# Hybrid encoder trunk on one core: in the dense heads, values copied out and normed in their own step, scaling moved ahead of the next combination, and a wait added to GpSimd's weight pieces

## What is computed

```python
def attend(q_blk):                                  # diff_attention, 128 queries at a time
    s = jnp.einsum('bqhcd,bkhcd->bhcqk', q_blk, k).astype(jnp.float32) * scale
    s = jnp.where(key_ok, s, NEG)
    p = jax.nn.softmax(s, axis=-1)
    a = p[:, :, 0] - lam * p[:, :, 1]
    return jnp.einsum('bhqk,bkhv->bqhv', a.astype(v.dtype), v)
...
    ob = diff_attention(qb, kb, vb, lam, valid)
    ob = rms_norm(ob, subln_w.reshape(B_HEADS, B_V_DIM)) * (1.0 - lam_init)
    yb = ob.reshape(bsz, lp, B_WIDTH).astype(dt) * jax.nn.silu(gb)
```

## Time and profile before

| | us |
|---|---|
| median of 3 runs | 1924.39 |
| lowest and highest run | 1917.27, 1925.56 |
| profiled execution, its own time | 1919.49 |
| its span | 1918.2 |
| busy: TensorE / VectorE / ScalarE / GpSimd | 1716.1 / 1107.8 / 878.5 / 406.7 |
| dense passes, layer 0 (B3 within) | about 570 to 875 (803 to 875) |
| dense passes, layer 1 (B3 within) | about 1506 to 1808 (1742 to 1808) |

### The profile page before, as it was taken

The page is one execution under the profiler, slowest core; times in us unless marked ns, Lnnn a source line. Parts: engine busy times, 40 slices in busy tenths (PEclk is TensorE's granted clock), DMA queues, the critical chain, the costliest instruction groups (busy, mean ns, idle before and its releaser), DMA issues.

```text
span 1918.2 us, 35760 instructions
## 1 busy us (share of the span) xinstructions
PE 1716.1 (89%) x13754; PEld 1591.9 (83%) x13754; DVE 1107.8 (58%) x2533; ACT 878.5 (46%) x2652; POOL 406.7 (21%) x390
## 2 busy tenths in 40 slices
PE   3799999999889899878989989999998888887896
PEld 3798899999888788668989989999998878775796
DVE  6475584445447777763185846834553575666516
ACT  4434545345416666572053444352552365546603
POOL 5430221220111102010463103113103101112044
PEclk9899999999989999899999999999998899999998
DMA  7200100200120111233031001011001111113312
GB/s 252 66 24 12 56 23 28 74 26 10 34 75 14 37 32 36 64 109 106 23 111 57 23 13 55 23 50 51 29 10 60 47 26 34 45 26 121 118 46 89
DMA packets 97705, 102.44 MB, mean 53 GB/s; under 512 B 7488, under 2 KB 87600, under 8 KB 97280
## 3 DMA queue, kind: packets, MB, share of 16 engines
q1 hardware_dynamic: 96576, 99.08, 16.0%
q10 hardware_dynamic: 960, 1.07, 0.2%
HBM read 70.43 MB, written 21.17 MB: 48 GB/s over the span
## 4 chain that ended last, share of the span: by engine, by line
PE 69%; DVE 16%; ACT 8%; issue 3%; POOL 2%; DMA 1%; SPq 0%; DVEq 0%; ACTq 0%
PE psum L855 45%; PE psum L995 6%; ACT p_b L1440 4%; PE psum L930 3%; PE psum L1142 3%; PE psum L1049 3%; DVE row_max L1909 3%; PE psum L1126 2%; DVE p_b L1923 2%; PE psum L1035 1%; DVE hbuf L1582 1%; ACT p_b L1438 1%; ACT aT_b L1450 1%; DVE stats L1575 1%; POOL w_lo L821 1%
## 5 line engine op out<-in xcount | busy, mean ns | idle before, releaser
L855 PE MATMUL psum<-w_hi,hT_hi 128*128 128x256 f32 x1824 | 529.6, 290 | 6.1 <-POOL w_lo L821 4.1
L855 PE MATMUL psum<-w_hi,hT_lo 128*128 128x256 f32 x1824 | 517.3, 284 | 0.0
L855 PE MATMUL psum<-w_lo,hT_hi 128*128 128x256 f32 x1824 | 516.8, 283 | 0.0
L817 POOL CAST w_hi<-w_raw 128x512 fp32r<-128x512 f32 (+1 forms) x168 | 112.7, 671 | 1354.9 <-DMA w_raw<-in_w_in 804.5
L855 PEld LDWEIGHTS psum<-w_hi,hT_hi 128*128 128x128 f32 x1824 | 348.0, 191 | 14.7 <-POOL w_lo L821 4.9
L855 PEld LDWEIGHTS psum<-w_lo,hT_hi 128*128 128x128 f32 x1824 | 348.1, 191 | 0.0
L855 PEld LDWEIGHTS psum<-w_hi,hT_lo 128*128 128x128 f32 x1824 | 348.1, 191 | 0.0
L855 PE MATMUL psum<-hT_hi,w_hi 128*128 128x346 f32 (+1 forms) x672 | 230.8, 343 | 24.2 <-DVE hT_lo L1568 9.3
L855 PE MATMUL psum<-hT_hi,w_lo 128*128 128x346 f32 (+1 forms) x672 | 222.2, 331 | 0.0
L855 PE MATMUL psum<-hT_lo,w_hi 128*128 128x346 f32 (+1 forms) x672 | 221.7, 330 | 0.0
L821 POOL TENSOR_TENSOR w_lo<-w_raw,w_hi 128x512 fp32r<-128x512 f32 (+1 forms) x168 | 211.3, 1258 | 34.4 <-DVE neg_max L1910 23.0
(11 more groups left out here) (161 smaller groups left out, 2661.7 us busy)
## 6 DMA issues: line engine op xcount, KB each, us to landing
w_raw<-in_w_in SPq DMA_DIRECT2D x72, 256.0 KB, 3.7
w_raw<-in_w_in SPq DMA_DIRECT2D x28, 512.0 KB, 4.2
h_dram<-hbuf SPq DMA_DIRECT2D x16, 512.0 KB, 2.6
w_raw<-in_w_out SPq DMA_DIRECT2D x16, 512.0 KB, 4.1
hbuf<-h_dram SPq DMA_DIRECT2D x16, 512.0 KB, 5.5
qk_b<-y_dram SPq DMA_DIRECT2D x16, 512.0 KB, 3.2
y_dram<-y_stage SPq DMA_DIRECT2D x96, 64.0 KB, 1.6
qk_t<-rot SPq DMA_DIRECT2D x56, 86.5 KB, 2.1
```

The source lines that it names most:

```text
L817: pool.tensor_copy(hi, raw).then_inc(w_hi_done, 1)
L855: last = nc.tensor.matmul(out_ap, lhs[a](k), rhs[b](k), start=k == 0 and a + b == 0, stop=k == KT - 1 and b == 1)
```

## The change

Three edits. On ScalarE, `norm` of step t now follows `values_out` of the same step, where before `norm` of t-1 stood ahead of it. On VectorE, `finish` of t-1 now stands ahead of `combine` of t+1 in all passes; in B3 it has also moved ahead of `lo_of_rows`. On GpSimd, the first operation of a piece tied to a pass now also waits for the combination of step j.

```diff
@@ gpsimd, beside_maximum
             step = b_step(l, head, n, 1)
             if c == 0:
+                pool.wait_ge(b_comb, B_STEP[l, head, n])
                 wait_filled(pool, ("s", l, *step, 1))
@@ scalar, pass_b
             def norm(step):
-                if step is None:
-                    return
                 g, t = step
...
-                norm(b_step(l, g, t, -1))
                 values_out(t)
+                norm((g, t))
                 if nx and t == q_tiles(l) - 2:
                     meta_out(l, nx)
                 if not nx and t >= Y_LAG:
                     hi_of_rows("y", l, t - Y_LAG)
-            if not nx:
-                norm((g, q_tiles(l) - 1))
@@ vector, pass_b
                 for x in made:
                     qk_rope(l, nx, x)
-                if not nx:
-                    if t > Y_LAG:
-                        lo_of_rows("y", l, t - 1 - Y_LAG)
-                    finish(b_step(l, g, t, -1))
+                finish(b_step(l, g, t, -1))
+                if not nx and t > Y_LAG:
+                    lo_of_rows("y", l, t - 1 - Y_LAG)
                 if after:
                     combine(after)
-                if nx:
-                    finish(b_step(l, g, t, -1))
```

## The result

The changed kernel takes 1893.07 us, the median of 4 runs (1886.95 to 1896.57). The kernel before, run beside it, takes 1922.57 (4 runs, 1917.27 to 1925.56). The ratio is 0.9846, with an interval from 0.9811 to 0.9881: 1.2 to 1.9% faster. The profiled execution took 1886.95 us with a span of 1885.6, 32.6 less than the span before. The forecast was 1901, with 1895 to 1907 as its own bounds and 1893 to 1910 as the range. So the direction was right and the gain larger than the sum said: 29.5 us between the medians instead of 23.4.

The account below looks back on a forecast made before the run. TensorE bounds steps with projections, rotations the ends of B1 and B2, a VectorE-ScalarE ring B3 and late B0. Gains of 7.8, 2.6, 7.7, 2.0 and 2.4 sum to 22.5 us, giving 1897.0 or 1901.9; forecast 1901, bounds 1895 to 1907, range 1893 to 1910.

Parts of the forecast that it names:

- the 0.44 us for L1910 beside a piece: B3, three pieces with a scaling, both layers: GpSimd's cast delays this tiny VectorE operation by 0.44, making steps 7.2 us.
- the 7.41 given to the first step of y's loop: B3 from step 4 on: every step that makes y takes 7.41 us, bounded by 6.95 and 7.7.
- the 0.4 for each late step of B0: B0: each late step gains 0.4 us, or 0.2 where rotations fill VectorE; B0 together 2.4.
- the hand-overs: At a pass's end TensorE runs without a gap, so the gain is not taken back there; no gain was summed.
- the plain ring: Undisturbed B3 steps: the loop through VectorE and ScalarE, from first maximum to first maximum, takes 6.75 us.
- the loop of the y steps: B3: maximum, `finish`, y's subtraction, transposes, values and scores take 7.41 us; 6.95 with `finish` behind the subtraction.
- Rival 1: GpSimd's piece takes the ports before `fscale`, which waits 0.9 us for six pieces: 3.7 us lost, 1905; chance 0.1.
- Rivals 2 and 4: 2: ScalarE or TensorE's clock is late next, 1913, chance 0.08; 4: combinations stay behind something else, 1916, chance 0.06.
- Rival 3: ScalarE's norm delays the copies that free TensorE in all 68 steps, deciding from 2.06 us on: 1938; chance 0.03.
- The step with the slow `fscale`: B0, layer 0: a GpSimd piece held `fscale` for 0.60 instead of 0.15 us; this step gains 0.8.
- the room beside TensorE: Projection steps: ScalarE has 2.06 us from the copy's start to its next copy; copy and norm take some 1.25.

Follow-up runs that it names:

- no_wait: The changed kernel without the new wait of GpSimd's pieces, both changes of order kept: 1898.4 us, 0.9884 of the kernel before.
- norm_longer: The changed kernel with nine further unused squares on ScalarE behind the norm in each step of B0 to B2: 1942.0 us, 1.0121 of the kernel before.
- t2_early: The changed kernel with y's subtraction ahead of `finish` in B3, and third transposes ahead of the projection in steps with one half: 1891.0 us, ratio 0.9849.
- wait_only: The kernel before with only the new wait of GpSimd's pieces added: 1914.8 us, 0.9964 of the kernel before.
- repeats: The changed kernel as it is, measured again in two other groups of runs: 1896.2 us (0.9873) and 1893.3 us (0.9872).
- act_only: The kernel before with only ScalarE's edit, the norm behind the copy of the same step: 1902.6 us, 0.9882 of the kernel before.
- nx_late: The changed kernel with `finish` behind the combination again in the passes with a next head, B3 untouched: 1900.2 us, 0.9882 of the kernel before.
- lo_first: The changed kernel with y's subtraction ahead of `finish` in B3: 1887.3 us, 0.9831 of the kernel before.

## Where the prediction held, and which of its steps failed

The mechanism held and the sizes failed. The steps that failed are three terms of the sum: the 0.44 us for L1910 beside a piece, the 7.41 given to the first step of y's loop, and the 0.4 for each late step of B0. The first two left 3.5 us of gain out, the third put 1.8 us too much in, and 2.6 us at the hand-overs were in no term. Of the profiled execution's distance some 6 us more lie in code that isn't changed.

**Right: what bounds B3 and what follows it.** The wait of 1.74 us for `rstd` is gone, the plain ring was put at 6.75 (its terms add up to 6.73) and takes 6.74, the loop of the y steps was put at 7.41 and takes 7.40 (6.95 with the subtraction first, as said, and measured). B1's steps kept TensorE full; B1 and B2 keep their lengths within 0.2 us in layer 0, and in layer 1 they are 0.9 shorter and 1.2 longer, where the changed kernel's own runs differ by 1.5 (B1). No combination is above 1.30. Rival 1 didn't happen (`fscale` takes 0.15); no_wait shows its collision where the wait is missing. Rivals 2 and 4 didn't happen either: the clock in B3 is 1.00, and the combinations stand behind nothing but the exponential. Rival 3 didn't happen, and norm_longer shows that it exists. One confirmation was luck: a late step of B0 took 7.20, and 7.20 - 0.45 for `finish` gave the ring's 6.75, but without `finish` it takes 7.12, since the copy of the third transposes holds it (t2_early).

**Failed: 0.44 for L1910 beside a piece.** The prediction said that the cast would hold the first `neg_max`, for 0.44 us. That price is right where the cast gets in first (0.42 in t2_early), and the earlier trace rows had read it rightly: there, at 1673.33, `neg_max` started 0.02 us behind the cast. Here it doesn't get in first. The cast (812.06) and `neg_max` (812.07) start within 0.01 us of each other, and `neg_max` takes 0.16. The subtraction holds the second one instead, for 0.68, but ScalarE wants that value only after the first exponential and the copy behind it, so 0.5 us of delay costs 0.08 (6.82 against 6.74). Six steps at 7.2 - 6.83: 2.2 us more gain than summed. Two things were not asked: by how little the cast is ahead, and which of the two `neg_max` is waited for at once.

**Failed: 7.41 for the first step of y's loop.** I gave 7.41 to all seven y steps. From the combination 4 to 5 it takes 6.74 in both layers, since the scores that this step's first maximum reads (822.56 in layer 0) stand behind the first y transposes (820.65), which wait for no bank: 2 x 0.67 = 1.3 us more; the last of layer 0 takes 7.26, another 0.15. Together B3 gave 23.8 instead of 20.1 (7.8 + 2.6 + 7.7 + 2.0).

**Failed the other way: 0.4 in B0.** I took 0.4 for each late step of B0, from an idle time of ScalarE. They give 0.08 (7.20 to 7.12): the wait ends on the transposes next (t2_early). The step with the slow `fscale` gives 0.52 (7.64 to 7.12), not 0.8: 0.09 from the wait (7.55 in wait_only), 0.35 because `finish` no longer meets the cast, and 0.08. Within the passes B0 to B2, counted from first to last combination of each, both layers came from 397.4 to 396.8 us: 0.6 instead of 2.4 (397.4 and 398.6 in the repeats, so even that is within the scatter). The last interval of every pass became some 0.46 shorter (7.80 to 7.33 in B1 of layer 0), which was in no term, and other short steps are made good by longer ones, since 7.98 and 9.14 became 7.58 and 9.53 in B1.

**Not in the sum: the hand-overs.** The prediction said only that TensorE runs without a gap there. Before, that is so in one of the six (from B2 to B3 in layer 0); in the others TensorE was busy for 85 to 92%. From the last combination of a head to the first of the next, the six of both layers took 62.0 us before and 59.4, 59.1 and 58.4 in the changed kernel's three runs. The kernels with `finish` behind the combination have 61.4, 60.4 and 64.0 (wait_only, act_only, nx_late), which speaks for the place of `finish`; no_wait has 60.1 and lo_first 60.9, where `finish` is ahead as well, and the clock in these stretches differs from run to run, as below. One hand-over tells them apart: from B1 to B2 in layer 0 it takes 9.8 to 10.5 us in the seven kernels and repeats that have the norm early and `finish` ahead (norm_longer left out), and 11.1 to 11.5 in the four with `finish` behind. But TensorE's granted clock there is 0.83 in six of the seven and 0.54 to 0.71 in the four, so whether the order acts by itself or through the clock isn't shown. Whether these 3 us are the change's stays open. That B0 to B2 with their hand-overs came out near the forecast (3.1 instead of 2.4) is luck.

**Read at the wrong place: the room beside TensorE.** The 2.06 us of the earlier trace rows ran to the next instruction of ScalarE. The point from which rival 3 decides is where TensorE needs that instruction's result, 3.4 us. So the rival was nearer in the prediction than in the kernel.

**The level.** The sum from the profiled execution gave 1897.0, and the changed kernel's took 1886.95: 3.7 of the difference of 10 are B3's, some 0.7 those of B0 to B2 with the hand-overs, and 5.7 lie in code that isn't changed. No term of the sum could have held those; the prediction had put the scatter at 4.

## What to carry to other kernels

An operation that waits costs what stands behind it on its queue: before moving one, look for the row behind it that frees another engine, as y's subtraction did; the same move of `finish` cost 40 us without the earlier norm. When a conflict of two engines can't be avoided, put it on the value that is wanted last: the same collision cost 0.67 us and more on the combination, 0.79 through `fscale`, 0.42 on the first `neg_max`, and 0.08 on the second. The idle time ahead of an instruction says how long it waited, not what shortening that wait is worth; the intervals between instructions that recur once a step say it to some 0.02 us, where the runs of one kernel lie up to 10 apart.

## What the chip showed that I had not expected

**A few hundredths of a microsecond decide at the shared ports.** In B3 of the changed kernel, in all six steps with a scaling, a cast of GpSimd's and the first `neg_max` start within 0.01 us of each other and take 0.64 (instead of 0.61) and 0.16: VectorE isn't held. With GpSimd's first by 0.02 `neg_max` takes 0.60, and by 0.03 `fscale` took 1.03 instead of 0.15. A tie doesn't always go to VectorE: in nx_late, at 1574.37 in both, VectorE's L1918 took 0.63 instead of 0.22. And the 0.14 us that a signal takes from VectorE to GpSimd are enough for the operation queued next on VectorE: a wait on the combination also protects what follows it directly, but not the third operation behind it (0.71 instead of 0.35 for the row of `finish` in nx_late).

**The same hand-over at three clocks.** The windows from the last combination of B2 to the first of B3 in layer 0, in the changed kernel's first and third profile:

```profile
784.69:795.85 11.16, 11.16 (x81) 8.75 (x81) 6.34 (x20) 4.71 (x19) 0.00 (x0) 0.54 0.07 18
```

```profile
787.61:796.50 8.89, 6.96 (x83) 5.55 (x83) 6.34 (x20) 5.08 (x21) 0.00 (x0) 1.00 0.09 19
```

The instructions are the same and VectorE's busy time is equal, but TensorE was granted 0.54 of its clock in one, nearly all of it at 1.2 GHz, and 1.00 in the other, and the stretch takes 11.16 or 8.89 us (11.35 at 0.70 in the second profile). TensorE ran without a gap in the slow one and was busy for 6.96 of 8.89 in the fast. Two such stretches in an execution are 4 to 5 us, as much as several of the kernels here differ by, and I have not found what decides them.
